# Moving every on-chip buffer of a float32 two-block transformer kernel to multiples of 1,024 bytes

## Chip, cores and metric

The kernel runs on one core of one Trainium2 chip. The metric is the device time of one execution, in microseconds (us). Most executions of a kernel of this kind agree within a few tenths of a per cent. The profile that is read here is that of one execution of the kernel before the change.

## The reference

The input is one sequence of 256 tokens with 2,048 features. It passes through two blocks, all in float32:

```python
def reference(x, ...):
    x = first_block(x, ...)
    return second_block(x, ...)

# first_block: rmsnorm, x @ w_in, dilated-window attention (16 heads) beside a gated
# linear attention in two directions, @ w_out, residual; then
#   h = rmsnorm(x, ffn_norm_w);  x = x + (silu(h @ w_gate) * (h @ w_up)) @ w_down;  rmsnorm
# second_block: scale and shift from c @ w_ada; rms_norm, x @ w_in_2, then retention,
# an RWKV-7 time mix and block-sparse attention side by side, @ w_out_2, gated residual; then
#   u = h @ w_ffn_up_2; a causal convolution of width 3; silu(gate) * val; @ w_ffn_down_2; rms_norm
```

The widths are 2,048 for the model and 5,632 for both feed-forward parts, so nearly all of the arithmetic lies in the products of 256 tokens with weight matrices, some 500 MB of float32 weights that are each read once.

## The kernel before

**Weights in two halves.** A product must have float32 accuracy, and the fast path of TensorE (type `fp32r`) keeps fewer bits. So each weight unit w of 128 partitions x 1,024 numbers is split: ScalarE writes `weights_hi`, w rounded to the short type (line 265), and VectorE writes `weights_lo` = w - `weights_hi` (line 272). Activations are split in the same way into `..._x_hi` and `..._x_lo`. Each product is then three matmuls: hi with hi, hi with lo, lo with hi.

**Rings.** SyncE loads weights by 1 MB into `raw_weights` (four slots of 2 units). The splits go into rings of four slots, `weights_hi` and `weights_lo`, and TensorE returns a slot by the semaphore `weights_used`. One loop of SyncE, ScalarE, VectorE and TensorE each runs through all units in the same order; ScalarE works three units ahead (`AHEAD`).

**Two shapes of matmul.** A matmul has a stationary operand (`lhsT`, 128 x 128, brought by a weight load, the rows PEld) and a moving operand (`rhs`), which streams through the array. In the form "T" the weights are stationary and the 256 tokens of an activation tile move (256 columns): the two feed-forward up projections (line 306), most of the first half of the input projections (lines 574 and 2084). In the form "rows" 128 tokens are stationary and 512 columns of the weight ring move: both down projections (lines 1762 and 1779), the value and output projections (the rest of lines 574 and 2084, and line 2360). Each matmul has its own weight load.

**The end of a down projection.** In `Down`, the last eight units are multiplied in another order (line 1779), and the last four of them lie in tiles of their own, `down_last_hi` and `down_last_lo`, not in the rings. So the code of line 1779 runs with moving operands from the ring for 24 matmuls, then with moving operands from `down_last` for 24, and this twice.

**Where the buffers begin.** The tiles of `Kit` are placed one behind the other by the allocator, from the first free byte of a partition. All other tiles are placed by hand with `at_byte` at a base plus a whole number of KB (1,024 bytes; lines 707, 2180, 3354 and 3571), and share one space with tiles of other stages. `x_at` is the address of `x_rows`, over which some tiles of the mixers are laid. With these rules the addresses of before, in bytes of a partition, are:

| buffers | start | modulo 512 |
|---|---|---|
| `x_rows` | 16,512 | 128 |
| `raw_weights` | 32,896 | 128 |
| `weights_hi`, `weights_lo` | 65,664 and 82,048 | 128 |
| `cst` (identity and constants) | 98,432 | 128 |
| first byte of the hand-placed space: activations, `ada_w`, `down_last_hi` and `_lo` | 110,784 | 192 |

Within a buffer every operand of these products begins at a whole number of 512 bytes: a ring slot has 4,096 bytes, the 512 moving columns 2,048, a stationary block of the ring 512; a row of an activation tile has 1,024 bytes, a stationary block of it 512.

Of the kernel before, what the change touches and what calls it, by code (L numbers as in the profile page):

```python
# [23 lines left out]
P = 128  # L24
# [30 lines left out]
UNIT = UK * UN // 2  # L55
SPLITS = 4
AHEAD = 3


COLS = {}  # L60
# [59 lines left out]
class Kit:  # L120


    def __init__(self, nc, ctx, ins, at):
        self.nc, self.ins, self.at = nc, ins, at
        self.ctx = ctx
        self.units = 0
        self.first_sems = []
        self.pairs = [0, 0]
        self.loads_done = 0
        self.norms = self.turned = 0  # L130
        self.dve_steps = 0
        self.act_steps = 0
        sb = self.sb
        self.x = sb("x_rows", [P, ST, D])
        self.x_at = -(-nc.sbuf_base // 32) * 32 - ST * D * 4
        self.raw = sb("raw_weights", [P, LOADS, 2 * UNIT])
        self.w_hi_t = sb("weights_hi", [P, SPLITS, UNIT], dt=R32)
        self.w_lo_t = sb("weights_lo", [P, SPLITS, UNIT], dt=R32)
        self.act_splits = self.ada_groups = 0
        self.resident = at["carry"][1]  # L140
        self.cst = sb("cst", [P, self.resident])
        self.col = sb("col", [P, NCOLS])
        self.stat = sb("stat", [P, 64])
        self.modT = sb("modT", [P, 2 * KT])
        self.modcols = sb("modcols", [P, 6 * D // P])
        self.ps = ctx.enter_context(nc.psum_tensor("ps", [P, 8, 512], F32))
        self.weights_in = [self.sem(f"weights_in{i}") for i in range(LOADS)]
        self.w_hi, self.w_lo, self.a_hi, self.a_lo = (
            self.sem(n) for n in ("weights_hi", "weights_lo", "act_hi", "act_lo"))
        self.ada_w = [self.sem("ada_w0"), self.sem("ada_w1")]  # L150
        self.ada_acc, self.ada_sum, self.ada_out = (self.sem("ada_" + n) for n in ("acc", "sum", "out"))
        self.weights_used = self.sem("weights_used")
        self.pair_free = [self.sem(f"pair_free{i}") for i in range(2)]
        self.dve_order = self.sem("dve_order")
        self.act_order = self.sem("act_order")
        self.loaded = self.sem("loaded")
        self.x_added, self.added = self.sem("x_added"), 0
        self.down_sums, self.down_out = self.sem("down_sums"), 0
        self.final_x, self.finals = self.sem("final_x"), 0
        self.cleared = self.sem("first_sems_cleared")  # L160
        self.n_mean = self.sem("norm_mean")
        self.n_rms = self.sem("norm_rms")
        self.s_recip, self.s_xT, self.s_xhi, self.s_xlo = (
            self.sem(n) for n in ("token_scales", "x_turned", "x_hi_out", "x_lo_out"))
        self.s_scaled = [self.sem(f"rows_scaled{t}") for t in range(ST)]
        self.s_mean0, self.s_root0, self.s_recip0 = (self.sem("first_half_" + n) for n in ("mean", "root", "recip"))
# [10 lines left out]
    def sb(self, name, shape, ctx=None, dt=F32):  # L177
        return (ctx or self.ctx).enter_context(self.nc.sbuf_tensor(name, shape, dt))
# [78 lines left out]
def split_hi(kit, act, n, i, m=None):  # L257


    m = n if m is None else m  # L260
    act.wait_ge(kit.weights_in[(m // 2) % LOADS], 16 * (m // (2 * LOADS) + 1) + 32 * i)
    if n >= SPLITS:
        act.wait_ge(kit.weights_used, n - SPLITS + 1 + 16 * i)
    raw = raw_half(kit, m)
    kit.nc.scalar.activation(kit.w_hi_t[:, n % SPLITS, :], raw, ACT.Copy).then_inc(kit.w_hi, 1)  # L265


def split_lo(kit, dve, n, i, m=None):

    dve.wait_ge(kit.w_hi, n + 1 + 16 * i)  # L270
    raw = raw_half(kit, n if m is None else m)
    kit.nc.vector.tensor_tensor(kit.w_lo_t[:, n % SPLITS, :], raw, kit.w_hi_t[:, n % SPLITS, :].bitcast(F32),  # L272
                                ALU.subtract).then_inc(kit.w_lo, 1)
# [344 lines left out]
class FirstMixer:  # L618
# [459 lines left out]
    def scalar(self, act):  # L1078
# [11 lines left out]
        for n in range(self.ticks):  # L1090
            split_hi(kit, act, n + AHEAD, 0)
            self.scalar_side(act, n)
# [135 lines left out]
    def vector(self, dve):  # L1228
# [12 lines left out]
        for n in range(self.ticks):  # L1241
            split_lo(kit, dve, n + AHEAD, 0)
            self.vector_side(dve, n)
# [289 lines left out]
class Glu:  # L1533
# [64 lines left out]
    def scalar(self, act):  # L1598
        kit, first = self.kit, self.first

        def body(i, j, half, _):
            for s in range(16):
                split_hi(kit, act, first + AHEAD + s, i)
                if isinstance(i, int) and i == 0:
# [8 lines left out]
    def vector(self, dve):  # L1613
# [5 lines left out]
        def body(i, j, half, summed):  # L1619
            for s in range(16):  # L1620
                begun = int(isinstance(i, int) and i == 0)
                split_lo(kit, dve, first + AHEAD + s, i)
                if begun:
# [21 lines left out]
class Down:  # L1645
# [220 lines left out]
    def ahead(self, p, i):  # L1866

        return None if not isinstance(i, int) else self.source(p + AHEAD)

    def scalar(self, act):  # L1870
# [3 lines left out]
        def tile(k, i):  # L1874
            if k >= 4:
                act.wait_ge(kit.weights_used, first + max(0, 2 * (k - R) + 2) + 16 * i)
            nc.scalar.activation(self.hi[k % R], self.act_tile(k, i), ACT.Copy).then_inc(kit.a_hi, 1)

        def body(k, i):
            for p in (2 * k, 2 * k + 1):  # L1880
                split_hi(kit, act, first + p + AHEAD, i, self.ahead(p, i))
            tile(k + 4, i)
# [1683 lines left out]
def program(nc, ins, at, out):  # L3566
    with ExitStack() as ctx:
        kit = Kit(nc, ctx, ins, at)
        mem = {"bias_dram": nc.dram_tensor("bias_rows", (AH, 2 * S), F32, kind="Internal")}
        base = -(-nc.sbuf_base // 32) * 32  # L3570
        t = lambda name, off, shape, dt=F32: kit.at_byte(name, base + off * 1024, shape, dt)
        tiles = lambda name, off: [t(f"{name}{n}", off + n, [P, S], R32)[:, :] for n in range(4)]
        ring = lambda x: [x[:, k, :] for k in range(4)]
# [113 lines left out]
```

## Time and profile before

| | |
|---|---|
| median of 3 runs | 2446.82 us (2445.85 to 2448.01) |
| profiled execution, first to last instruction (its own time; no other is given for it) | 2445.8 us |
| TensorE matmul busy | 2425.4 us, 99% |
| TensorE weight load busy | 2205.9 us, 90% |
| VectorE busy | 1621.5 us, 66% |
| ScalarE busy | 1149.9 us, 47% |
| DMA | 541 MB, 63% of the time of 16 engines |

Matmuls are pipelined: one that the profile gives 279 ns ends after the next has begun. What a matmul costs in a row of matmuls is therefore the distance between the starts of two neighbours, which this text calls the cadence. A piece of the chain that ended last, such as "90.46 PE ps L306 x768", gives it directly: 90.46 us over 768 matmuls.

### The profile page before, as it was taken

How to read it: one execution, taken by the hardware profiler on the slowest of the kernel's cores; microseconds unless marked ns; L12 is line 12 of the kernel's file. 1: busy time of each engine (PE TensorE's matmuls, PEld its weight loads, DVE VectorE, ACT ScalarE, POOL GpSimd, SP SyncE). 2: the span in 40 equal slices, each digit the busy share in tenths (PEclk: the TensorE clock that was granted, in tenths of full speed). 3: DMA queues.
4: the chain of work that ended last, by engine and by line, in shares of the span. 5: the costliest groups of instructions: out<-in, count | busy, mean ns of one | idle time of the engine just before them, and what ended most of it. 6: DMA issues, size and time to landing. Idle time of an engine off the chain costs nothing.

```text
span 2445.8 us, 43133 instructions
## 1 busy us (share of the span) xinstructions
PE 2425.4 (99%) x18001; PEld 2205.9 (90%) x18001; DVE 1621.5 (66%) x1962; ACT 1149.9 (47%) x1516; POOL 0.3 (0%) x5
## 2 busy tenths in 40 slices
PE   9999999999999999999999999999999999999998
PEld 8889778999999998888899898988999999998886
DVE  5568457777777766777777455566878756664456
ACT  5465344534334334444664344445544444554444
POOL 0000000000000000000000000000000000000000
PEclk9999999999999999999999999999999999999999
DMA  8555467778777766888476344455677655555553
GB/s 280 171 170 182 150 225 268 268 263 289 275 265 285 272 238 251 317 312 293 154 279 242 125 142 139 139 185 195 245 271 258 224 207 189 190 203 193 188 187 121
DMA packets 214566, 541.27 MB, mean 221 GB/s; under 512 B 9130, under 2 KB 15860, under 8 KB 202516
## 3 DMA queue, kind: packets, MB, share of 16 engines
q1 hardware_dynamic: 214420, 539.18, 63.0%
q8 instruction: 110, 1.80, 0.3%
q14 instruction: 36, 0.29, 0.0%
HBM read 533.86 MB, written 5.28 MB: 220 GB/s over the span
## 4 chain that ended last, share of the span: by engine, by line
PE 97%; DVE 1%; ACT 1%; DMA 0%; issue 0%; SPq 0%; DVEq 0%; ACTq 0%
PE ps L306 36%; PE ps L1762 18%; PE ps L574 18%; PE ps L2084 15%; PE ps L1779 2%; PE ps L2602 0%; DMA raw_weights<-in_w_in_dram 0%; PE ps L2360 0%; PE ps L2621 0%; PE ps L974 0%; PE ps L1004 0%; PE ps L432 0%; PE ps L2616 0%; PE ps L986 0%; PE ps L1016 0%
## 5 line engine op out<-in xcount | busy, mean ns | idle before, releaser
L272 DVE TENSOR_TENSOR weights_lo<-raw_weights,weights_hi 128x1024 fp32r<-128x1024 f32 x786 | 957.9, 1224 | 745.4 <-ACT weights_hi L265 741.5
L265 ACT ACTIVATE weights_hi<-raw_weights 128x1024 fp32r<-128x1024 f32 x782 | 827.0, 1061 | 1182.0 <-PE ps L306 459.2
L485 DVE SCALAR_TENSOR_TENSOR ada_acc<-ada_w,col,ada_acc 128x1024 f32<-128x1024 f32 x180 | 230.1, 1278 | 0.1
L306 PE MATMUL ps<-glu_x_hi,weights_hi 128*128 128x256 f32 x1280 | 202.8, 280 | 0.0
L306 PE MATMUL ps<-glu_x_lo,weights_hi 128*128 128x256 f32 x1280 | 202.5, 279 | 0.0
L306 PE MATMUL ps<-glu_x_hi,weights_lo 128*128 128x256 f32 x1280 | 202.5, 279 | 0.0
L306 PE MATMUL ps<-conv_x_hi,weights_hi 128*128 128x256 f32 x1280 | 198.8, 277 | 0.0
L306 PE MATMUL ps<-conv_x_hi,weights_lo 128*128 128x256 f32 x1280 | 197.9, 277 | 0.0
L306 PE MATMUL ps<-conv_x_lo,weights_hi 128*128 128x256 f32 x1280 | 197.9, 277 | 0.0
L306 PEld LDWEIGHTS ps<-glu_x_lo,weights_hi 128*128 128x128 f32 x1280 | 173.2, 188 | 0.0
L306 PEld LDWEIGHTS ps<-glu_x_hi,weights_hi 128*128 128x128 f32 x1280 | 173.1, 188 | 0.0
L306 PEld LDWEIGHTS ps<-glu_x_hi,weights_lo 128*128 128x128 f32 x1280 | 173.0, 187 | 0.0
L306 PEld LDWEIGHTS ps<-conv_x_hi,weights_hi 128*128 128x128 f32 x1280 | 169.7, 188 | 1.0 <-issue 1.0
L306 PEld LDWEIGHTS ps<-conv_x_hi,weights_lo 128*128 128x128 f32 x1280 | 169.5, 188 | 0.0
L306 PEld LDWEIGHTS ps<-conv_x_lo,weights_hi 128*128 128x128 f32 x1280 | 169.5, 188 | 0.0
L2084 PE MATMUL ps<-m_x_hi,weights_hi 128*128 128x256 f32 (+1 forms) x576 | 96.4, 289 | 0.6 <-issue 0.3
L3555 DVE SCALAR_TENSOR_TENSOR conv_y<-ps,conv_taps,conv_y 128x255 f32<-128x255 f32 (+1 forms) x176 | 72.5, 475 | 28.1 <-ACT conv_y L3491 27.2
L1762 PE MATMUL ps<-weights_hi,down_hi 128*128 128x512 f32 x288 | 90.8, 396 | 0.3
L2084 PE MATMUL ps<-m_x_hi,weights_lo 128*128 128x256 f32 (+1 forms) x576 | 90.7, 279 | 0.0
L2084 PE MATMUL ps<-m_x_lo,weights_hi 128*128 128x256 f32 (+1 forms) x576 | 90.7, 279 | 0.0
L1762 PE MATMUL ps<-weights_hi,down_lo 128*128 128x512 f32 x288 | 90.5, 395 | 0.0
L1762 PE MATMUL ps<-weights_lo,down_hi 128*128 128x512 f32 x288 | 90.5, 395 | 0.0
(531 smaller groups left out, 3688.2 us busy)
## 6 DMA issues: line engine op xcount, KB each, us to landing
raw_weights<-in_w_in_dram SPq DMA_DIRECT2D x99, 1024.0 KB, 5.3
ada_w<-in_w_ada_dram SPq DMA_DIRECT2D x96, 1024.0 KB, 6.9
raw_weights<-in_w_ffn_up_dram SPq DMA_DIRECT2D x88, 1024.0 KB, 5.3
raw_weights<-in_w_gate_dram SPq DMA_DIRECT2D x44, 1024.0 KB, 5.1
raw_weights<-in_w_up_dram SPq DMA_DIRECT2D x44, 1024.0 KB, 5.1
raw_weights<-in_w_down_dram SPq DMA_DIRECT2D x44, 1024.0 KB, 5.4
raw_weights<-in_w_ffn_down_dram SPq DMA_DIRECT2D x44, 1024.0 KB, 4.8
raw_weights<-in_w_out_dram SPq DMA_DIRECT2D x32, 1024.0 KB, 5.1
```

Source lines behind the costliest of these rows:

```text
L265: kit.nc.scalar.activation(kit.w_hi_t[:, n % SPLITS, :], raw, ACT.Copy).then_inc(kit.w_hi, 1)
L272: kit.nc.vector.tensor_tensor(kit.w_lo_t[:, n % SPLITS, :], raw, kit.w_hi_t[:, n % SPLITS, :].bitcast(F32), ALU.subtract).then_inc(kit.w_l ...
L306: ins = nc.tensor.matmul(out, lhsT=lhsT, rhs=rhs, start=start and m == 0, stop=(k == KT - 1 and m == 2), skip_group_check=True)
L485: step = nc.vector.scalar_tensor_tensor(acc, w, c, acc, ALU.mult, ALU.add)
L574: ins = nc.tensor.matmul(out, lhsT=lhsT, rhs=rhs, start=start and m == 0, stop=ends and m == 2, skip_group_check=True)
L1762: ins = nc.tensor.matmul(kit.ps[:, 4 * t + 2 * half + q, :], lhsT=lhsT, rhs=rhs, start=(k == 0 and m == 0), stop=ends and m == 2, skip_gro ...
L1779: ins = nc.tensor.matmul(kit.ps[:, 4 * t + 2 * half + q, :], lhsT=lhsT, rhs=w[:, q * UN:(q + 1) * UN], start=False, stop=k == w_tiles - 1 ...
L2084: ins = nc.tensor.matmul(out, lhsT=lhsT, rhs=rhs, start=start and m == 0, stop=ends and m == 2, skip_group_check=True)
L3555: nc.vector.scalar_tensor_tensor(y[:, j, q, b:S], self.tile(j, q)[:, 0:S - b], taps[:, j, tap, q:q + 1], y[:, j, q, b:S], ALU.mult, ALU.ad ...
```

## The change

`base`, from which all hand-placed tiles count, is rounded up to 1,024 bytes in place of 32, and a tile `head_room` of 896 bytes a partition, which nothing reads or writes, is placed ahead of `x_rows`.

```diff
+ALIGN = 1024
...
         sb = self.sb
+        sb("head_room", [P, (-(-nc.sbuf_base // 32) * -32 % ALIGN) // 4])
         self.x = sb("x_rows", [P, ST, D])
         self.x_at = -(-nc.sbuf_base // 32) * 32 - ST * D * 4
...
-        base = -(-nc.sbuf_base // 32) * 32
+        base = -(-nc.sbuf_base // ALIGN) * ALIGN
         t = lambda name, off, shape, dt=F32: kit.at_byte(name, base + off * 1024, shape, dt)
```

`x_rows` now begins at 17,408, `raw_weights` at 33,792, `weights_hi` at 66,560, `weights_lo` at 82,944, `cst` at 99,328 and the hand-placed space at 112,640: all multiples of 1,024. The distance of ring and activations, taken modulo 512, goes from 64 to 0. Only `col`, `stat`, `modT`, `modcols` and a few tiles of under 200 bytes begin elsewhere, as before.

Each engine has the same instructions in the same order as before, with the same semaphores; the line numbers grow by 1 or 2. DMAs move the same bytes.

## Rows read from the trace of the kernel before

**Rows 1.** The page, part 1: busy time by engine.
```profile
PE 2425.4 (99%) x18001; PEld 2205.9 (90%) x18001; DVE 1621.5 (66%) x1962; ACT 1149.9 (47%) x1516; POOL 0.3 (0%) x5
```
**Rows 2.** Chain that ended last, whole span: shares by line.
```profile
by line: PE ps L306 36.3%; PE ps L1762 18.2%; PE ps L574 18.2%; PE ps L2084 15.1%; PE ps L1779 1.8%; PE ps L2602 0.5%; DMA raw_weights<-in_w_in_dram 0.5%; PE ps L2360 0.5%; PE ps L2621 0.4%; PE ps L974 0.3%; PE ps L1004 0.3%; PE ps L432 0.3
```
**Rows 3.** The same chain's long pieces: start us, us, what, count.
```profile
488.12 48.05 PE ps L306 x408
537.05 90.46 PE ps L306 x768
...
902.37 42.40 PE ps L306 x360
944.80 224.24 PE ps L1762 x960
...
1748.93 70.67 PE ps L306 x600
1821.32 108.80 PE ps L306 x960
1931.84 257.15 PE ps L306 x2269
```
**Rows 4.** Timeline of PE, 1171 to 1185 us: start us, us, matmuls.
```profile
1174.01 0.63 PE L1779 MATMUL ps<-weights_hi,glu_x_lo 128*128 128x512 f32 x2
...
1175.86 0.61 PE L1779 MATMUL ps<-down_last_hi,glu_x_hi 128*128 128x512 f32 x2
...
1179.49 0.62 PE L1779 MATMUL ps<-down_last_hi,glu_x_lo 128*128 128x512 f32 x2
...
1180.41 0.63 PE L1779 MATMUL ps<-weights_lo,glu_x_hi 128*128 128x512 f32 x2
...
1184.61 0.63 PE L1779 MATMUL ps<-weights_lo,glu_x_hi 128*128 128x512 f32 x2
```
**Rows 5.** Chain, 100 to 240 us: two pieces of equal work.
```profile
121.44 5.45 PE ps L574 x48
...
131.37 5.66 PE ps L574 x48
```
**Rows 6.** Groups by line and shape: busy us, mean ns, idle before.
```profile
L574 PE MATMUL ps<-weights_hi,m_x_hi 128*128 128x512 f32 x256 | 83.1, 406 | 0.0
...
L574 PE MATMUL ps<-m_x_hi,weights_lo 128*128 128x256 f32 x384 | 60.5, 279 | 0.0
...
L574 PE MATMUL ps<-weights_hi,m_a_hi 128*128 128x512 f32 x64 | 20.8, 406 | 0.0
L574 PE MATMUL ps<-glu_x_hi,weights_hi 128*128 128x256 f32 x128 | 20.5, 281 | 0.0
```
**Rows 7.** The page, part 5: the 256-wide group of line 2084.
```profile
L2084 PE MATMUL ps<-m_x_hi,weights_lo 128*128 128x256 f32 (+1 forms) x576 | 90.7, 279 | 0.0
```
**Rows 8.** Waits: who waited for whom, us in total, times, longest.
```profile
ACT weights_hi L265 <- PE ps L306: 459.2, 274, 3.4
...
PE ps L574 <- DVE weights_lo L272: 0.4, 1, 0.4
```
**Rows 9.** Windows: window, PE busy (matmuls), clock, DMA share, GB/s.
```profile
1174.50:1179.90 5.40, 5.40 (x25) 1.00 1.00 378
```
**Rows 10.** Windows of all engines: PE, PEld, DVE, ACT, POOL, clock, DMA share, GB/s.
```profile
1000.00:1100.00 100.00, 100.00 (x430) 80.60 (x429) 77.22 (x78) 43.22 (x53) 0.00 (x0) 1.00 0.85 312
600.00:700.00 100.00, 100.00 (x852) 100.00 (x851) 71.60 (x60) 39.22 (x38) 0.00 (x0) 1.00 0.77 272
2000.00:2100.00 100.00, 100.00 (x885) 100.00 (x884) 62.14 (x81) 48.86 (x56) 0.00 (x0) 1.00 0.57 199
```
**Rows 11.** Chain, 0 to 40 us: the first load, and four transposes.
```profile
6.42 11.44 DMA raw_weights<-in_w_in_dram
...
24.14 0.44 PE ps L834 x4
```
**Rows 12.** Chain, 1700 to 1940 us: four transposes of the second block.
```profile
1707.13 0.44 PE ps L2013 x4
```

## Prediction, made before the changed kernel was run

> **What bounds the kernel now.** I read the busy times first: TensorE's matmuls are busy for 99% of the span, VectorE for 66%, ScalarE for 47% [rows 1]. Then the chain of work that ended last: five lines of matmuls hold 89.6% of it, 36.3 + 18.2 + 18.2 + 15.1 + 1.8 [rows 2]. Then the waits: ScalarE waits for TensorE to give a slot back (459.2 us for line 306 alone), and TensorE waits for a split weight once, for 0.4 us [rows 8]. So the time is that of a row of matmuls, and an edit without new or moved instructions can matter only by changing the cadence, or by making the feeding so slow that TensorE waits.
>
> **The cadence isn't one number.** It is the thing to look at, since a moved buffer can touch nothing else of TensorE. Long pieces of the chain, divided by their matmuls [rows 3]:
> - line 306, 256 columns: 90.46 us / 768 = 117.8 ns, and the same in all six pieces from 488.12 to 902.37 (3,840 matmuls) and in the 600 from 1748.93. But 108.80 / 960 = 113.3 ns and 257.15 / 2,269 = 113.3 ns behind them, with the same code, the same tiles, and at the full granted clock in both [rows 10].
> - line 1762, 512 columns: 224.24 / 960 = 233.6 ns.
> - line 574: 48 matmuls take 5.45 us in one place, 5.66 in another, 113.5 and 117.9 ns [rows 5].
>
> So there are two steady speeds for 256 columns, 4.44 ns apart, and a stretch keeps the one that it begins with until something interrupts it. Other engines don't set it: the windows at 600 and 2000 us have VectorE at 72 and 62% and DMA at 272 and 199 GB/s, and the starts inside each stretch are equal to the nanosecond's rounding.
>
> **One place of the trace has the offset that the change makes.** Weight ring and activations lie 64 bytes apart modulo 512. The tiles `down_last` are hand-placed like the activations, so there the distance is 0, as it is everywhere after the change. The timeline of line 1779 [rows 4] has both, one after the other, with the same stationary tile:
> - moving operand from the ring: up to 1174.01, and again 1180.41 to 1184.61, 18 matmuls in 4.20 us, 233.3 ns;
> - moving operand from `down_last`: 1175.86 to 1179.49, 16 matmuls in 3.63 us, 226.9 ns.
>
> It goes back to 233.3 with the ring and comes down again with the next `down_last` tiles, in both down projections; in the second the first dozen still take about 230. The clock is 1.00 in the fast stretch, and DMA is at 378 GB/s, more than at 1000 us, where the ring's speed holds [rows 9, 10]: neither is the reason. And 226.7 is twice 113.3: it looks as if 113.3 ns for each 256 columns were the free speed, and 117.8 and 233.3 that speed with some cycles lost where the weight load's reads and the moving reads meet.
>
> **The change part by part.**
> 1. *512-wide matmuls of ring weights*, 6.6 to 6.7 ns each. Line 1762: 18.2% of 2,445.8 us [rows 2] is 445 us, less 2.86% (226.67 against 233.33): 12.7 us. Line 574: three groups of 256 and three of 64 [rows 6] are 960 matmuls: 6.4 us. Line 2084: 15.1% of the span is 369 us; three groups of 576 at 256 columns [rows 7] take 1,728 x 117.5 ns = 203 us of it, and the other 166 us are about 710 of 512: 4.7 us. Line 2360 and the ring part of 1779 (48 and 96): 1.0. Sum 24.8 us.
> 2. *256-wide, line 306*: 3,840 + 600 matmuls at 117.8 come to 113.3: 4,440 x 4.44 ns = 19.7 us. The 3,240 at 113.3 stay.
> 3. *256-wide, lines 574 and 2084*: three groups of 384 and six of 128 [rows 6], with the 1,728 of line 2084, are 3,648. Of their distances between starts 2,765 lie near 118 ns and 773 near 113; rows 5 have one piece of each kind. That is 78%, 2,850 x 4.44 ns = 12.7 us.
> 4. *Plain float32 matmuls and transposes*: nothing. Four transposes take 0.44 us whether their moved tile is `x_rows`, at distance 0 from the constants, or a hand-placed one at 64 [rows 11, 12].
> 5. *Splits and other work of VectorE and ScalarE*: the trace has no pair that differs in this alone. It lies under TensorE; if TensorE becomes 2.5% faster, VectorE's fullest stretch goes from 77% to 79% [rows 10]. Bounds 0 and 0.
> 6. *Loads*: the fullest stretch goes from 312 GB/s to 321 [rows 10], and 378 has been reached [rows 9]. Only the first load is uncovered, 11.44 us [rows 11]. Between nothing and a tenth of it, 0 to -1.1; I take 0.
>
> Sum of 1 to 3: 57.2 us. Some is not reached, since a stretch that begins badly needs a dozen matmuls to come down, as the second `down_last` stretch did, and about a hundred stretches are shorter than 50 matmuls: I take off 2 us. Against the profiled 2,445.8 us this is 2,390.6. That execution stands 1.0 us under the median of the runs, so 2,391.6.
>
> What I don't know is whether point 2 and 3 follow. The `down_last` rows show distance 0 for moving weights and stationary activations only. In the other form the roles are exchanged, and there even a distance of 64 allows the free speed.
>
> **What a rule says against it.** The Trainium skill, "TensorE: Matmul & The Clock Gate", Step-by-step: what each phase is for, has the moving operand and the weight load on two independent read ports, so that loading doesn't take read bandwidth from the running matmul; by it no distance between the two matters and the change is worth 0. Rows 4 don't agree. The same page, Back-to-back issue gap, gives N / 2.4 + 2.5 ns, 109.2 and 215.8 ns for 256 and 512 columns; no stretch of this trace reaches them, and a kernel that did would be, as an estimate by that page, about 145 us faster.
>
> **The rivals.**
> - *Only the 512-wide ones gain* (0.22). The 256-wide form has two speeds by how a stretch begins, and goes on having them: 2,446.8 - 24.8 = 2,422. The long stretches may also change sides: line 306's fast 3,240 becoming slow costs 14.4 us, the first block's slow 3,840 becoming fast gives 17.1. So 2,405 to 2,437. For it: rows 5, the same operands at both speeds.
> - *No change* (0.16), 2,445 to 2,449: `down_last` is fast for another reason, such as lying in a part of the memory that nobody writes then, or not being split into just before. Against it: the ring speed is the same to 0.1 ns at all loads of the other engines. This is also where the port rule of the page above ends up.
> - *Slower* (0.17): with stationary blocks of the ring and moving activations at distance 0 the two reads meet at every weight load. Line 1762 shows what that costs: 6.67 ns a weight load over the free speed. The 256-wide matmuls, 7,680 + 3,648 + 48 of lines 306, 574, 2084 and the gate codes (line 558), then go to 113.3 + 6.7 = 120.0 ns. Their mean is now (7,290 x 117.8 + 4,090 x 113.3) / 11,380 = 116.2. This costs 11,380 x 3.8 ns = 43 us, less the 24.8 of point 1: +18.5 us, 2,465. It decides from a mean of 116.2 + 24.8 / 11.38 = 118.4 ns on.
> - *Still faster* (0.03): round addresses free cycles that no row here has free; under 2,384.
>
> **How the numbers follow.** The forecast, all three gains, has 0.42, and its own range is 2,386 to 2,400. Of the rest, a mixture that changes sides can also make "no change" faster or slower by more than 0.2%, about 5 us, which is what a measurement of this kernel can tell. Faster: 0.42 + 0.22 + 0.03, less a little of the mixture that comes out even: 0.66. Same: 0.14. Slower: 0.20, the slow rival and 0.03 for the mixture. A range from 2,384 to 2,452 leaves out the slow rival and the still faster one.
>
> **What would show it.** In the profile after: pieces of line 306 near 0.1133 us a matmul in both blocks, of line 1762 near 0.2267; line 1779 with one cadence throughout; about 57 us less in those lines and the idle times of TensorE as before. Points 2 and 3 are wrong if a long piece of line 306 has 117.8 or more; point 1 is wrong if line 1762 keeps 233.6. The whole is wrong if TensorE begins to wait for `weights_lo` or for `raw_weights`.

## The result, and the profile after

The changed kernel takes 2464.44 us (median of 4 runs, 2463.65 to 2465.38) against 2446.34 of the kernel before: a ratio of 1.0073, with an interval of 1.0059 to 1.0087. It is slower by 0.7%, clear of the interval, where 2,391.6 us, 2.3% less, was forecast. The span of the profiled execution goes from 2,445.8 to 2,462.0 us.

The page of the changed kernel, part 1, has TensorE as full as before [rows 1], its weight loads (PEld) busy for 39.7 us more, and the other engines within 2.4 us of where they were:

```profile
PE 2443.5 (99%) x18001; PEld 2245.6 (91%) x18001; DVE 1621.9 (66%) x1962; ACT 1152.3 (47%) x1516; POOL 0.3 (0%) x5
```

The long pieces of the chain of the changed kernel answer to [rows 3] (line numbers are 2 higher; start us, us, what, count):

```profile
536.39 92.15 PE ps L308 x768
...
951.65 217.83 PE ps L1764 x960
...
1748.94 72.00 PE ps L308 x600
1822.66 115.19 PE ps L308 x960
1939.57 272.18 PE ps L308 x2269
```

Divided out: the 512-wide matmuls of line 1764 come from 233.6 to 226.9 ns, as forecast. The 256-wide of line 308 go to 120.0 ns (92.15 / 768, 115.19 / 960, 272.18 / 2,269), from 117.8 in the first block and from 113.3 in the second. There is one speed for them now. In line 576 the two kinds of piece of [rows 5] have become one (chain of the changed kernel, 100 to 240 us):

```profile
121.42 5.74 PE ps L576 x48
...
131.67 5.75 PE ps L576 x48
```

The timeline of line 1781, which had two cadences in [rows 4], has one, 0.45 us for two matmuls with either moving operand:

```profile
1179.75 0.62 PE L1781 MATMUL ps<-down_last_hi,glu_x_lo 128*128 128x512 f32 x2
1180.20 0.62 PE L1781 MATMUL ps<-weights_hi,glu_x_hi 128*128 128x512 f32 x2
1180.65 0.61 PE L1781 MATMUL ps<-weights_lo,glu_x_hi 128*128 128x512 f32 x2
```

The groups by shape show that the weight loads of the 256-wide matmuls have become longer too, 192 ns against 187 or 188 before, while those of the 512-wide ones stay at 188. The first line is that of the kernel before, the others are those of the changed kernel:

```profile
L306 PEld LDWEIGHTS ps<-glu_x_hi,weights_lo 128*128 128x128 f32 x1280 | 173.0, 187 | 0.0
...
L308 PEld LDWEIGHTS ps<-glu_x_hi,weights_lo 128*128 128x128 f32 x1280 | 176.6, 192 | 0.0
...
L1764 PEld LDWEIGHTS ps<-weights_lo,down_hi 128*128 128x128 f32 x288 | 54.1, 188 | 11.2
```

To size both effects, take every distance between the starts of two neighbouring matmuls, from 100 to 130 ns for 256 columns and from 180 to 245 ns for 512, and add up what each is above 113.3 or 226.7 ns, the lowest steady cadences seen. The 256-wide matmuls stood 32.2 us above before and stand 73.6 above now: +41.4 us. The 512-wide ones stood 24.3 us above and stand 2.5 above: -21.8. Together that is +19.6 against +16.2 of the span. Of the 3.4 us between the two, 1.15 are the first load, 10.29 us in the chain in place of 11.44 [rows 11], and the rest is not traced to a place. The first load isn't the change's doing, since it took 9.6 to 10.9 in every later kernel, also with `raw_weights` where it lay before (10.20 in acts_only).

### The profile page after: what moved, and what is told of

It is laid out like the page before. It is cut to its first block, busy times and chain, and to the rows that moved or that the text cites. A ratio compares the mean times of both kernels' runs of the same rounds, so it can differ in the third digit from the quotient of the medians.

```text
span 2462.0 us, 43133 instructions
## 1 busy us (share of the span) xinstructions
PE 2443.5 (99%) x18001; PEld 2245.6 (91%) x18001; DVE 1621.9 (66%) x1962; ACT 1152.3 (47%) x1516; POOL 0.3 (0%) x5
## 4 chain that ended last, share of the span: by engine, by line
PE 97%; DVE 1%; ACT 1%; DMA 0%; issue 0%; SPq 0%; DVEq 0%; ACTq 0%
PE ps L308 37%; PE ps L576 18%; PE ps L1764 18%; PE ps L2086 15%; PE ps L1781 2%; PE ps L2604 0%; PE ps L2362 0%; DMA raw_weights<-in_w_in_dram 0%; PE ps L2623 0%; PE ps L976 0%; PE ps L1006 0%; PE ps L434 0%; PE ps L2618 0%; PE ps L988 0%; PE ps L1018 0%
## 5 line engine op out<-in xcount | busy, mean ns | idle before, releaser
L274 DVE TENSOR_TENSOR weights_lo<-raw_weights,weights_hi 128x1024 fp32r<-128x1024 f32 x786 | 958.3, 1224 | 757.5 <-ACT weights_hi L267 755.0
L267 ACT ACTIVATE weights_hi<-raw_weights 128x1024 fp32r<-128x1024 f32 x782 | 828.8, 1061 | 1192.5 <-PE ps L308 486.6
L308 PE MATMUL ps<-conv_x_hi,weights_hi 128*128 128x256 f32 x1280 | 206.6, 284 | 0.0
L308 PE MATMUL ps<-conv_x_lo,weights_hi 128*128 128x256 f32 x1280 | 205.8, 283 | 0.0
L308 PE MATMUL ps<-conv_x_hi,weights_lo 128*128 128x256 f32 x1280 | 205.8, 283 | 0.0
L308 PEld LDWEIGHTS ps<-conv_x_hi,weights_hi 128*128 128x128 f32 x1280 | 176.8, 192 | 1.0 <-issue 1.0
L308 PEld LDWEIGHTS ps<-conv_x_hi,weights_lo 128*128 128x128 f32 x1280 | 176.6, 192 | 0.0
L308 PEld LDWEIGHTS ps<-conv_x_lo,weights_hi 128*128 128x128 f32 x1280 | 176.6, 192 | 0.0
L3557 DVE SCALAR_TENSOR_TENSOR conv_y<-ps,conv_taps,conv_y 128x255 f32<-128x255 f32 (+1 forms) x176 | 72.7, 475 | 33.2 <-ACT conv_y L3493 32.4
```

The lines of the kernel that those rows point to most:

```text
L308: ins = nc.tensor.matmul(out, lhsT=lhsT, rhs=rhs, start=start and m == 0, stop=(k == KT - 1 and m == 2), skip_group_check=True)
L3557: nc.vector.scalar_tensor_tensor(y[:, j, q, b:S], self.tile(j, q)[:, 0:S - b], taps[:, j, tap, q:q + 1], y[:, j, q, b:S], ALU.mult, ALU.ad ...
```

## Experiments

All kernels but narrow_rows and the three last differ from the changed kernel only in where the two groups of buffers begin. With "rings" go `x_rows`, `raw_weights`, `weights_hi`, `weights_lo` and `cst`; "activations" are the hand-placed tiles.

```diff
-ALIGN = 1024
+RING_AT, ACTS_AT = 0, 64                      # zero_64; other pairs in the others
...
-        sb("head_room", [P, (-(-nc.sbuf_base // 32) * -32 % ALIGN) // 4])
+        sb("head_room", [P, (RING_AT - -(-nc.sbuf_base // 32) * 32) % 1024 // 4])
...
-        base = -(-nc.sbuf_base // ALIGN) * ALIGN
+        base = -(-nc.sbuf_base // 32) * 32
+        base += (ACTS_AT - base) % 1024
```

In acts_only there is no `head_room`. Every ratio is that to the kernel before, timed again beside the run, so it need not be the quotient of two medians given here.

### Is it the address or the distance

**both_192** (192, 192):

> Weight rings and activations both begin at 192 modulo 1,024: the distance between them is 0 as in the changed kernel, but no address is a round one. Theory D (the distance between stationary and moving operand, modulo some power of two, sets the cadence): 256-wide matmuls at 120.0 ns, 512-wide at 226.7 ns, time 2464 us as the changed kernel. Theory A (the address of each operand by itself sets it, a moving activation tile at 0 being bad): activations lie where they lay before, so the 256-wide ones keep 113.3 or 117.8 ns, the 512-wide take 226.7 as down_last at 192 did, 2422 us.

Measured: 2464.18 us, ratio to before 1.0079 (1.0062 to 1.0096). Its chain has the pieces of the changed kernel:

```profile
536.96 92.15 PE ps L308 x768
...
952.22 217.83 PE ps L1764 x960
```

**zero_64** (0, 64):

> Rings at 0 modulo 1,024, activations at 64: the distance of the kernel before at other addresses. Theory D: the kernel before again, 233.3 ns for 512 columns, 113.3 or 117.8 ns for 256, 2446 us within what the mixture of the two speeds can shift (2430 to 2461). Theory A: the moving rings at 0 go with 226.7 ns (25 us less than before) and the activations at a new address are open, 2422 if they keep their mixture.

Measured: 2445.39 us, ratio 1.0004 (0.9994 to 1.0013). Its chain has the pieces of the kernel before, up to which of the two speeds each stretch has:

```profile
536.51 90.46 PE ps L308 x768
...
944.27 224.23 PE ps L1764 x960
...
1819.29 108.80 PE ps L308 x960
```

Theory D holds in both and theory A in neither: round addresses do nothing, the distance between ring and activations does. All addresses tried here, round or not, are multiples of 64 bytes.

**ring_only** (0, 192), one part of the change alone:

> One part of the change alone: x_rows, the rings and constants move to multiples of 1,024, the hand-placed tiles stay at 192 modulo 512. Theory A: the 512-wide matmuls, whose moving operand is the ring, gain the full 25 us, the 256-wide, whose moving operand has not moved in phase, stay: 2422 us. Theory D: the distance is 192, which no row has shown; both cadences may be new, and equal to those of any other kernel with distance 192.

Measured: 2426.47 us, ratio 0.9925 (0.9909 to 0.9942), faster than both kernels. Line 1764 comes down, but not to 226.9: 219.99 / 960 = 229.2 ns. Line 308 keeps both speeds.

```profile
529.90 90.46 PE ps L308 x768
...
937.65 219.99 PE ps L1764 x960
...
1803.80 108.83 PE ps L308 x960
```

**acts_only** (128, 0), the other part alone:

> The other part alone: only the hand-placed tiles move to a multiple of 1,024, rings stay at 128 modulo 512. Theory A: 256-wide matmuls, whose moving tile now begins at 0, take 120.0 ns, and the 512-wide keep 233.3: 2446 plus 43 is 2489 us. Theory D: the distance is -128 (384 modulo 512), not seen so far; the 256-wide and 512-wide cadences need not be those of the changed kernel, and 2489 would be a coincidence.

Measured: 2470.45 us, ratio 1.0103 (1.0086 to 1.0120). Line 307 takes 91.14 / 768 = 118.7 ns in both blocks (113.92 / 960 in the second), line 1763 takes 233.6 in the first block and 219.16 / 942 = 232.7 in the second. The expectation by theory A, 2489 us, fails here too. So the two parts alone do -0.75% and +1.03% and together +0.73%: they can't be added, since each changes the distance.

### The period, and finer steps

**zero_128**, **zero_256**, **zero_320**, **zero_448**:

> Rings at 0 modulo 1,024, activations at 128. The distance sets the cadence by now; open is its period and which is best. If the period is 256, this is the same as activations at -128 from the rings: 118.7 ns for 256 columns, about 232.9 for 512, 2470 us. If the period is 512, it lies between distance 64 and 192: 113.3 or 117.8 ns and 229 to 233 ns, 2425 to 2446 us.

> Rings at 0 modulo 1,024, activations at 256. Period 256 (or 128, 64): as distance 0, 120.0 ns and 226.7 ns, 2464 us. Period 512: something else, and a chance of the free speeds for both forms (113.3 and 226.7 ns, 2391 us).

> Rings at 0 modulo 1,024, activations at 320. Period 256: as distance 64, 113.3 or 117.8 ns and 233.3 ns, 2446 us within the mixture. Period 512: something else.

> Rings at 0 modulo 1,024, activations at 448, that is -64. Period 256: as distance 192, 113.3 or 117.8 ns and 228.9 ns, 2426 us. Period 512: something else.

Measured: 2470.22 us (1.0107, 1.0077 to 1.0136), 2465.09 (1.0086, 1.0056 to 1.0115), 2442.87 (1.0000, 0.9989 to 1.0011) and 2424.50 (0.9920, 0.9891 to 0.9949). All but zero_320 (eight runs) rest on two runs each. Each takes the cadences of its partner at the distance 256 bytes away, for both shapes; at 128 the 512-wide matmuls take 232.6 ns, which acts_only shows in its second block only. So the cadences repeat every 256 bytes, and the table below excludes a smaller period.

**zero_32**, **zero_160**, **zero_224**:

> Rings at 0 modulo 1,024, activations at 32. If the loss is counted in lines of 64 bytes, one of its neighbours: 120.0 and 226.7 ns (2464 us) or 113.3 or 117.8 and 233.3 (2446). If it is finer, something between, possibly free for both forms, 2391 us.

> Rings at 0 modulo 1,024, activations at 160. In lines of 64 bytes: as 128 (118.7 and 232.4 ns, 2470 us) or as 192 (228.9 ns and 113.3 or 117.8, 2425 us). Finer: between the two, 2425 to 2470.

> Rings at 0 modulo 1,024, activations at 224. In lines of 64 bytes: as 192 (2425 us) or as 256 (120.0 and 226.7 ns, 2464 us). Finer: the loss of the 512-wide form falls from 5.3 to 0 cycles on this stretch, that of the 256-wide rises from 0 or 10.7 to 16; the best point of both may lie here, 2410 to 2425 us.

Measured: 2452.33 us (1.0031, 1.0020 to 1.0042), 2469.48 (1.0095, 1.0066 to 1.0125) and 2469.57 (1.0096, 1.0066 to 1.0125). The guess for zero_224, that the best point lies there, is a miss, and none of the three is better than 192. The steps between multiples of 64 follow no single rule. At 224 the 512-wide matmuls lose about the full 6.7 ns, though at 192 and 0 they lose 2.5 and nothing; at 32 they lose as much as at 64. The 256-wide ones at 160 vary from stretch to stretch.

The whole map, from the chain pieces of line 308 (768 in the first block, 960 in the second) and of line 1764 (first 960), in ns a matmul:

| activations minus ring, modulo 256 | 256 columns | 512 columns | time, us |
|---|---|---|---|
| 0 (changed, both_192, zero_256) | 120.0 | 226.9 | 2464.4, 2464.2, 2465.1 |
| 32 (zero_32) | 116.7 | 233.6 | 2452.3 |
| 64 (before, zero_64, zero_320) | 117.8 or 113.3 | 233.6 | 2446.3, 2445.4, 2442.9 |
| 128 (acts_only, zero_128) | 118.7 | 233.6, 232.6 | 2470.5, 2470.2 |
| 160 (zero_160) | 117.3 to 120.0 | 233.6 | 2469.5 |
| 192 (ring_only, zero_448) | 117.8 or 113.3 | 229.2 | 2426.5, 2424.5 |
| 224 (zero_224) | 118.3 | 233.6 | 2469.6 |

### Why the two shapes want different distances

**narrow_rows**, the changed kernel with line 1764 moving 256 columns at a time (its line 1765):

```diff
                 for m in range(3):
-                    for q in range(2):
-                        wh, wl = (x[:, s, q * UN:(q + 1) * UN] for x in (kit.w_hi_t, kit.w_lo_t))
+                    for q in range(4):
+                        wh, wl = (x[:, s, q * S:(q + 1) * S] for x in (kit.w_hi_t, kit.w_lo_t))
                         lhsT, rhs = ((h, wh), (h, wl), (l, wh))[m]
-                        ins = nc.tensor.matmul(kit.ps[:, 4 * t + 2 * half + q, :], lhsT=lhsT, rhs=rhs,
-                                               start=(k == 0 and m == 0), stop=ends and m == 2, skip_group_check=True)
+                        out = kit.ps[:, 4 * t + 2 * half + q // 2, (q % 2) * S:(q % 2 + 1) * S]
+                        ins = nc.tensor.matmul(out, lhsT=lhsT, rhs=rhs, start=(k == 0 and m == 0 and q % 2 == 0),
+                                               stop=ends and m == 2, skip_group_check=True)
```

> The changed kernel (distance 0) with one edit: line 1764 moves 256 columns of the ring a matmul in place of 512, so twice the matmuls and weight loads, activations still stationary. Theory N (it is the number of moving columns for each weight load that decides: 256 with one load lose 16 cycles, 512 lose none): 120.0 ns a matmul, line 1764 takes 1920 x 2 x 120.0 = 461 us in place of 435, the kernel 2490 us. Theory R (the roles decide: stationary weights of the ring lose, stationary activations don't): 113.3 ns a matmul, the kernel stays at 2464 us.

Measured: 2490.91 us in its one run. Its chain and its groups by shape:

```profile
951.80 230.61 PE ps L1765 x1920
```
```profile
L1765 PEld LDWEIGHTS ps<-weights_hi,down_lo 128*128 128x128 f32 x576 | 79.5, 192 | 0.0
```

230.61 / 1,920 = 120.1 ns, with ring weights moving and activations stationary, and the weight loads take 192 ns as in line 308. The forecast of theory N, 2490 us, holds: at distance 0 it is the number of columns that move for each weight load that decides, not which operand does. This was tried at distance 0 alone. At any other distance the exchange of roles also turns the distance round: counted from the stationary operand to the moving one, the 64 of the table is 64 for the 256-wide matmuls and 192 for the 512-wide. So away from 0 the table doesn't separate the number of columns from the sign of the distance.

### What picks one of the two speeds

The three last are built on zero_448. They add something behind the eight transposes (`turned`) that interrupt the first block's up and gate projections six times; the results go to bank 4 of PSUM and nothing reads them.

```diff
-            mid = (lambda: self.ada.turned(pe, self.lead, j)) if summed else None
+            def mid():
+                self.ada.turned(pe, self.lead, j)
+                keep_busy(kit, 1, 4)                       # flip_t1; 2 in flip_t2
+            mid = mid if summed else None
...
+                kit.nc.tensor.matmul(kit.ps[:, 4, :], lhsT=kit.c("ones"), rhs=kit.cst[:, 0:UN], start=True, stop=True)   # flip_row, in place of keep_busy
```

> Rings at 0, activations at 448 modulo 1,024 (distance 192 of the period of 256), and one more transpose of 128 columns behind each of the six ada transposes groups in the first block's gate and up projections, whose 3,840 matmuls of line 308 stood at the slow one of the two speeds, 117.8 ns. Theory P (which speed a stretch takes is set by the instant at which its reads begin against the weight loads, so by what ran just before it): some stretch changes to 113.3 ns, up to 17 us faster, 2408 us. Rival F (the speed is a property of the first block's tiles and addresses): all stay at 117.8, 2425 us.

> The same with two more transposes in place of one. Theory P: another draw, each stretch at 113.3 or 117.8 ns, 2408 to 2425 us. Rival F: all stay at 117.8, 2425 us.

> The same with one plain float32 matmul of 512 columns in place of the extra transpose, the kind of matmul (line 3408 of the kernel before) behind which the second block's stretches went to 113.3 ns in every kernel with distance 64 or 192. Theory P: the first block's stretches go to 113.3 ns, 17.1 us less and 0.75 us more for each of six extra matmuls, 2412 us. Rival F: 117.8 remains, 2429 us.

Measured: 2424.31 us (ratio to before 0.9922, 0.9905 to 0.9938), 2418.53 (0.9896, 0.9880 to 0.9913) and 2416.53 (0.9892, 0.9875 to 0.9908). Pieces of the chain in the first block, of zero_448, flip_t1, flip_t2 and flip_row in this order:

```profile
712.43 90.46 PE ps L308 x768
803.76 90.46 PE ps L308 x768
895.09 42.40 PE ps L308 x360
```
```profile
530.56 87.08 PE ps L308 x768
618.62 90.46 PE ps L308 x768
```
```profile
618.78 87.07 PE ps L308 x768
706.95 90.46 PE ps L308 x768
798.50 87.07 PE ps L308 x768
```
```profile
709.78 87.07 PE ps L308 x768
798.58 87.07 PE ps L308 x768
887.39 40.83 PE ps L308 x360
```

87.07 / 768 = 113.4 ns, 90.46 / 768 = 117.8. Of the four stretches of 768, zero_448 has all at the slow speed. One more transpose turns the first of them, two turn the first, second and fourth, a 512-wide float32 matmul turns all four and the 360 behind them. Same tiles, same addresses, same matmuls in the stretch: rival F falls. What runs just before a stretch can change its speed, which is what theory P asks; that the instant of the first reads is what counts, as P has it, is argued and not shown.

The gain is smaller than the stretches give. flip_row was to save 12.6 us (17.1 less 4.5) and saves 8.0 against zero_448, though the turned stretches give 4 x 3.39 + 1.57 = 15.1. Three things were not in the forecast, or not at this size:
- Each interruption has grown from 803.76 - (712.43 + 90.46) = 0.87 us to 798.58 - (709.78 + 87.07) = 1.73 us; six times 0.86 are 5.2. The profile shows the added matmul as two, 431 ns each.
- The 408 matmuls ahead of the first long stretch keep 48.05 us. No addition stands directly ahead of them, but 240 matmuls of line 576 at 117.8 ns (28.27 us).
- In the second block, where nothing was added, 240 matmuls of line 576 and the 600 of line 308 behind them were fast in zero_448 and are slow in flip_row, 3.7 us in all. 15.1 less 5.2 and 3.7 is 6.2; the two profiled executions differ by 2421.6 - 2414.5 = 7.1.

```profile
1704.58 27.22 PE ps L576 x240
1731.79 68.00 PE ps L308 x600
```
```profile
1693.69 28.27 PE ps L576 x240
1721.96 70.67 PE ps L308 x600
```

The last point says more: the 600 go on at the speed of the 240 ahead of them, over the change of line. And ring_only, which has zero_448's distance and its instructions to the last one, takes 70.67 us for the same 600. So neither the distance nor the order of instructions alone fixes the speed. flip_t1 has these 600 at 70.67 us too, and with one stretch turned it is no faster than zero_448. Only one execution of each kernel was profiled, and no run shows whether a stretch has the same speed in each execution.

## Why the prediction was wrong

- **What bounds the kernel**: right. The cadence of the matmuls accounts for +19.6 us where the span grew by 16.2. TensorE doesn't begin to wait: its matmuls waited for `weights_lo` once before, 0.4 us, and not at all after, and its weight loads 0.5 us in all after.
- **Point 1, the 512-wide matmuls, -24.8 us**: right, -21.8 measured. The missing 3 us lie in the short stretches of lines 576 and 2086, whose mean is 228.2 ns in place of 226.7: what was written of stretches that need a dozen matmuls to come down, and sized at 2 us.
- **Points 2 and 3, the 256-wide matmuls, -19.7 and -12.7 us**: this is the step that failed. It read "226.7 is twice 113.3", took distance 0 to be where nothing is lost, and carried what `down_last` showed for 512 moving columns over to 256. They lose 6.7 ns a matmul there (120.0 - 113.3; 16 cycles at the full granted clock, 2.4 GHz), more than the 0 or 4.4 of the old distance, and together they cost 41.4 us in place of saving 32.4. The halving was wrong too: narrow_rows moves the same ring weights 256 columns at a time and takes 120.1 ns, not 113.3.
- **The slow rival, 2,465 us at 0.17**: it is what happened, with its place, its 120.0 ns a matmul and its sum (measured 2464.4). Its ground was wrong: it blamed the exchanged roles, and narrow_rows has the same loss with the roles of `down_last`. That the size came out is luck: 6.67 ns was read from 512 columns at distance 64, and for 256 columns the loss is 5.4 ns at distance 128 and 5.0 at 224. The chance was too low, since the prediction itself said that the rows showed one form only, and the other form held 11,380 of some 15,100 ring matmuls.
- **"Only the 512-wide gain"**: not this change, but near what ring_only and zero_448 do at distance 192, where the 512-wide matmuls gain 4.4 of the 6.7 ns.
- **"No change", and the port rule behind it**: wrong. By the Trainium skill, "TensorE: Matmul & The Clock Gate", Step-by-step: what each phase is for, the weight load takes nothing from the running matmul, since each has its own read port. The trace doesn't agree: here the distance between what the two read moves the matmul from 113.3 to 120.0 ns, and the weight load from 188 to 192.
- **The two speeds**: that a stretch keeps the speed with which it begins was right. flip_t1 to flip_row add that what ran just before can change it.
- **Splits and loads**: right at nothing. VectorE's split stays at 1,224 ns, ScalarE's at 1,061; the median landing of the input weights goes from 5.3 to 5.2 us. That of the first block's down projection goes from 5.4 to 6.7, and TensorE doesn't wait for it.

That the two read streams of TensorE meet somewhere in the memory is argued from the distance and from its period of 256 bytes. The weight load adds little: it takes 192 ns where a matmul takes 120.0 at distance 0, but stays at 188 where one takes 118.7 (distance 128) or 233.6. No run shows the place where they meet. Why 256 columns at distance 64 and 192 allow two speeds and at 0 one, and why the steps of 32 bytes follow no single rule, stays open too. Distances that are no multiple of 32 were not tried, nor a layout that gives each shape its own distance.

## What to carry to other kernels

Where matmuls with a weight load each bound a kernel, read the cadence from long pieces of the chain, per shape, and compare stretches of the same shape; two values there are worth more than any busy share. Don't round addresses for their own sake: choose the distance between stationary and moving buffers by trying it, here in steps of 64 over 256 bytes (no step of 32 was better), and count for each shape apart, because the best for one can be the worst for another. A comparison that one trace happens to offer, as `down_last` did, holds for its own shape until another shape is tried.

## What was not expected of the hardware

- The distance of two buffers modulo 256 bytes changes a 256-column fp32r matmul from 113.3 to 120.0 ns and a 512-column one from 226.7 to 233.6, and a whole kernel of this kind by 1.9% (2424.5 to 2470.5 us), with not one instruction changed. The addresses themselves, multiples of 64 in the runs that compare them, do nothing.
- The same matmuls on the same tiles run at 113.3 or 117.8 ns for hundreds in a row (2,269 at 113.3, 768 at 117.8), and 0.11 us of a transpose ahead of them was enough to change one stretch of 768 (flip_t1); 0.86 us of another matmul changed all five stretches that follow one (flip_row).
- The kernel with the lowest median, flip_row, adds six matmuls whose result nothing reads, and is 1.1% faster than the kernel before (2416.53 us, 0.9892). flip_t2 (0.9896) can't be told from it.
